# Start of the expert stages: logits with tokens on the partitions, x parts kept in x's order, the first gather split around the first gate products

## The chip, the cores and the metric

One core of one Trainium2 chip. The metric is the time of one execution on the device in microseconds; the median of the runs counts.

## The reference, cut to what matters

A network of four layers on x with 256 tokens of 1024 features, all in float32: two layers of a mixer and a mixture of experts, then two of a pooling mixer with dense feed-forward parts. The change concerns the mixture of experts of the first two:

```python
def _hier_moe(x, w_grp, b_grp, w_exp, b_exp, w_gate, w_up, w_down):
    grp_logits = (xf @ w_grp + b_grp).astype(F32)          # 4 groups
    g_idx = jnp.argmax(grp_logits, axis=-1)
    exp_logits = (xf @ w_exp + b_exp).reshape(n, N_GROUPS, EXPERTS_PER_GROUP)
    top_l, top_e = lax.top_k(in_grp, TOP_K_IN_GROUP)       # 2 of the 8 of the group
    gate = p_grp[:, None] * jax.nn.softmax(top_l, axis=-1)
    ...
    hdn = jax.nn.silu(xb @ w_gate[e]) * (xb @ w_up[e])     # 1024 -> 512
    return hdn @ w_down[e]                                 # 512 -> 1024
```

## The kernel before, in words

**Sizes.** Tokens stand in two blocks `tb` of 128, features in eight tiles of 128 (`KT`). Products that need more precision than one rounded pass split each operand into a high part (rounded, float32r) and a low part (the rest): ScalarE writes the high one, VectorE the low one, and three products are summed. `x_tok` has tokens on the partitions, `xT_parts` (`xh`, `xl`) is x turned, in parts.

**Order of the work.** Each engine runs a stream written out by hand (`pe_program`, `act_program`, `dve_program`, `pool_program`, `sp_program`, in three blocks with a barrier of all engines after pair 7 of each expert stage). Engines wait for each other by semaphores (`S.name[key]`). `Banks.open` takes the next PSUM bank of a group in turn and waits until its last user was evacuated: `A_BANKS` is 0 and 1, `B_BANKS` 4 to 7.

**From the mixer to the experts (layers 0 and 1).** VectorE normalizes block 0 and then block 1 into `x_tok`. TensorE turns each block by eight transposes (`transpose_x_pe`, L479), with four products that nobody reads ahead of block 1 (`busy_pe`, L460, 128x512 in full float32, two records each). ScalarE copies the turned halves to `xh` (L495), VectorE writes `xl` (L504). ScalarE also writes the high part of `x_tok` (`token_part_act`, L1252) in an order in which the eight features of a group are apart (`by_kk`), VectorE the low part (`token_parts_dve`, L1263). `route_pe` then computes the logits with the router weights (36 columns padded to 128) as the stationary operand and 256 tokens moving, 24 products; VectorE copies them (L1162), TensorE turns them (L1110), and a chain of small VectorE operations picks group and experts (L1165 to L1178), TensorE counts places (from `chosen_hot`), with five busy products ahead. `select_dve` (L1277) makes a 0/1 matrix `sel` that places the tokens of four experts.

**Gather (`gather_pe`).** For two pairs of experts at once, x is gathered by 32 products in four banks `q`, with the parts of `x_tok` as stationary operand and `sel` moving. ScalarE evacuates banks 0 and 2 (L1317), VectorE 1 and 3 (L1332). Then `sel` is turned (L1301) and the pair's weights are placed (`weights`). There are eight gathers in a layer; the first of a block stands ahead of its first pair.

**Pair `g` (`experts_pe`).** Gate products in two halves of four feature tiles (`paired_pe`, L1345; two experts in two column halves of the array), up products alike, the hidden rows turned (L1405), down products in two halves, and the last pair's result combined. Each half gives two weight chunks back.

**Weights.** `loads_sp` issues chunks of 1 MB in the order of use (L358), each when the last user of its slot is done; in an expert stage there are 16 slots (7 of the ring, 9 lent, the areas of `xh`, `xl` and `x_tok` among them). A pair has 12 chunks.

Of the kernel before, what the change touches and what calls it, by code (L numbers as in the profile page):

```python
# [465 lines left out]

def transpose_x_pe(e, k, n, after=None):
    S = k.S
    for tb in range(NB):
        if n < 0:  # L470
            e.wait_ge(*S.x_loaded[tb][0])
        for half in range(2):
            view = pairs(k.banks.open(e, B_BANKS, ("xT", n, tb, half))[:, :], 4)
            if n >= 0 and half == 0:
                busy_pe(e, k, k.banks["xT", n, tb, half], BUSY[after][tb])
            if n >= 0:
                e.wait_ge(*S.x_tok[n, tb, half])
            for i in range(4):
                ins = e.transpose(view[:, i, :], k.x_tok[:, tb, block(4 * half + i)], k.ident)  # L479
            ins.then_inc(*S.turned.tell((n, tb, half)))  # L480
# [617 lines left out]

def route_pe(e, k, layer, n):
    S, R = k.S, k.route  # L1100
    _, hi, lo = split_views(k, ("router", layer))
    bank = k.banks.open(e, A_BANKS, ("logits", layer))
    e.wait_ge(*S.low["router", layer])
    x_ready(e, k, n, 1)
# [6 lines left out]
    ins.then_inc(*S.product.tell(("turned_logits", layer)))  # L1111
# [10 lines left out]
def route_turned(k, bank):  # L1122
    return pairs(bank[:, 0:NB * N_LOGITS])
# [18 lines left out]
def route_dve(e, k, layer):  # L1142
# [17 lines left out]
    token_parts_dve(e, k, layer)  # L1160
    e.wait_ge(*S.used["router", layer])
    e.tensor_copy(k.rot_tmp[0:n, 0:T], k.banks["logits", layer][0:n, 0:T]).then_inc(*S.dve_out.tell(("logits", layer)))  # L1162
    view = route_turned(k, k.banks["turned_logits", layer])
    e.wait_ge(*S.product["turned_logits", layer])
    e.tensor_tensor(R.gl, view[:, :, 0:N_GROUPS], mid_bcast(k.b_grp[:, layer, :], NB), ALU.add).then_inc(*step.tell(("group_logits", layer)))  # L1165
    e.tensor_tensor(R.el, view[:, :, N_GROUPS:n], mid_bcast(k.b_exp[:, layer, :], NB), ALU.add).then_inc(*S.dve_out.tell(("turned_logits", layer)))
# [5 lines left out]
    e.wait_ge(*S.dve_out["turned_logits", layer])  # L1172
# [86 lines left out]
def token_parts_dve(e, k, layer):  # L1259
    S = k.S  # L1260
    for tb in range(NB):
        e.wait_ge(*S.token_high[layer, tb])
        e.tensor_tensor(k.x_tok_low[:, tb, :, :], by_kk(k.x_tok[:, tb, :]), k.x_tok_high[:, tb, :, :].bitcast(F32), ALU.subtract  # L1263
                        ).then_inc(*S.token_low.tell((layer, tb)))
# [21 lines left out]
def gather_pe(e, k, X, G):  # L1286

    S, b = X.S, k.experts
    for q in range(KT // 2):
        view = pairs(X.banks.open(e, B_BANKS, X.key("xg", G, q))[:, :])  # L1290
# [6 lines left out]
        ins.then_inc(*S.product.tell(X.key("gather", G, q)))  # L1297
    view = pairs(X.banks.open(e, B_BANKS, X.key("selT", G))[:, :], GATHERED)
# [36 lines left out]
def paired_pe(e, k, X, tiles, name, g, per, lhs):  # L1335

    for half in range(2):
# [48 lines left out]
def experts_pe(e, k, X, first, last):  # L1386
    S, b = X.S, k.experts
    gather_pe(e, k, X, first // GATHERED)
    for g in range(first, last):
        xg = b.xg[:, :, places(g % GATHERED)]  # L1390
        gate = X.banks.open(e, (0,), X.key("silu", g))
        if g % GATHERED == 0:
            e.wait_ge(*S.act_out[X.key("xg", g // GATHERED, 2)])
            e.wait_ge(*S.dve_out[X.key("xg", g // GATHERED, 3)])
        paired_pe(e, k, X, [gate], "gate", g, KT // 2, xg)
        up = X.banks.open(e, (1,), X.key("h", g))
        paired_pe(e, k, X, [up], "up", g, KT // 2, xg)
        if gathered_after(g, last) is not None:
            gather_pe(e, k, X, gathered_after(g, last))
# [16 lines left out]
def experts_act(e, k, X, first, last, ahead=None):  # L1416

    S, b = X.S, k.experts
    gather_act(e, k, X, first // GATHERED)
    for g in range(first, last):  # L1420
# [1525 lines left out]
```

## Time and profile before

| | |
|---|---|
| Median of 3 runs | 2324.59 us (2318.47 to 2326.11) |
| The profiled execution | span 2323.1 us from its first to its last instruction |
| TensorE busy | 2166.1 us, 93% |
| VectorE busy | 1142.2 us, 49% |
| ScalarE busy | 784.0 us, 34% |
| Moved | 622.66 MB, mean 268 GB/s |

The time of the profiled execution itself is not given beside its span; the span lies 1.5 us under the median. Busy TensorE is the time in which any matmul record is open. Two records that overlap on the array are counted once. Windows and timelines give microseconds from the first instruction.

### The profile page before, as it was taken

To read this page: it belongs to the slowest core of one execution; us is meant where nothing else is said; L and a number is where in the kernel's file an instruction comes from. 1 tells how busy PE (TensorE), PEld (TensorE's weight loads), DVE (VectorE), ACT (ScalarE), POOL (GpSimd) and SP (SyncE) were. 2 spreads that over 40 slices of the span, in tenths; PEclk is the share of its full clock that TensorE was granted. 3 is DMA by queue.
4 is the path that set the end of the run, shared out by engine and by line. 5 is a ranking of instruction groups with operands and counts; after the bars stand their busy time and mean duration, and the time that the engine had idled before them with its cause. 6 is when DMAs were issued, how large, how long until landed. Compare 5 with 4: busy or idle time off the path is not lost.

```text
span 2323.1 us, 30109 instructions
## 1 busy us (share of the span) xinstructions
PE 2166.1 (93%) x12126; PEld 1528.0 (66%) x12126; DVE 1142.2 (49%) x1786; ACT 784.0 (34%) x1299; POOL 61.5 (3%) x62
## 2 busy tenths in 40 slices
PE   8999998899887989997988999999999999989998
PEld 7884443443367944433433688898888788888887
DVE  5582222121156831211111666678666766787666
ACT  3441110111034321101111355454555455554553
POOL 0010000000010100000000000001000000001000
PEclk9999999899998799999999999999999999999999
DMA  9449999999972289999999864634555464534561
GB/s 289 145 175 379 421 421 421 417 421 420 413 246 73 76 363 420 420 421 415 420 420 421 295 209 168 199 128 127 181 200 200 154 208 166 193 96 159 167 208 46
DMA packets 231542, 622.66 MB, mean 268 GB/s; under 512 B 15456, under 2 KB 166944, under 8 KB 182112
## 3 DMA queue, kind: packets, MB, share of 16 engines
q1 hardware_dynamic: 226096, 605.32, 68.7%
q0 software_dynamic: 3040, 10.78, 1.5%
q10 hardware_dynamic: 2256, 4.50, 0.5%
q8 instruction: 102, 1.67, 0.3%
q14 instruction: 48, 0.39, 0.0%
HBM read 619.51 MB, written 1.05 MB: 267 GB/s over the span
## 4 chain that ended last, share of the span: by engine, by line
PE 41%; DMA 6%; DVE 4%; ACT 2%; issue 1%; POOL 0%; SPq 0%; DVEq 0%; ACTq 0%
PE bank L1517 14%; PE bank L1505 10%; PE bank L1518 7%; PE bank L228 6%; PE bank L1345 3%; DMA arena<-in_moe_w_up 1%; DMA ring<-in_moe_w_up 1%; DMA ring<-in_ffn_gate 1%; DMA w_parts<-in_moe_w_up 1%; DMA x_tok<-in_moe_w_up 1%; DVE w_low L439 1%; PE bank L1673 1%; ACT w_high L432 1%; DVE x_tok L687 0%; DVE x_tok L676 0%
## 5 line engine op out<-in xcount | busy, mean ns | idle before, releaser
L439 DVE TENSOR_TENSOR w_low<-ring,w_high 128x1024 fp32r<-128x1024 f32 x364 | 441.1, 1225 | 271.7 <-ACT w_high L432 271.7
L1517 PE MATMUL bank<-xT_parts,w_high 128*128 128x512 f32 x1408 | 496.2, 395 | 6.0 <-DVE xT_parts L504 6.0
L432 ACT ACTIVATE w_high<-ring 128x1024 fp32r<-128x1024 f32 x364 | 377.1, 1053 | 218.0 <-PE bank L1518 184.6
L1518 PE MATMUL bank<-xT_parts,w_low 128*128 128x256 f32 x1408 | 394.5, 280 | 0.0
L1345 PE MATMUL bank<-ring,arena 128*64 128x512 f32 x1344 | 339.0, 594 | 17.3 <-DMA w_parts<-in_moe_w_gate 5.3
L1517 PEld LDWEIGHTS bank<-xT_parts,w_high 128*128 128x128 f32 x1408 | 264.0, 188 | 69.0 <-DVE xT_parts L504 6.9
L1345 PE MATMUL bank<-w_parts,arena 128*64 128x512 f32 x768 | 263.8, 609 | 13.4 <-DMA w_parts<-in_moe_w_up 6.7
L1518 PEld LDWEIGHTS bank<-xT_parts,w_low 128*128 128x128 f32 x1408 | 265.8, 189 | 3.1
L1345 PEld LDWEIGHTS bank<-ring,arena 128*64 128x64 f32 x1344 | 110.1, 137 | 230.5 <-issue 221.9
L1453 DVE SCALAR_TENSOR_TENSOR arena<-arena,bank 128x512 f32<-128x512 f32 x32 | 23.9, 747 | 434.1 <-PE bank L1345 434.1
L228 PE MATMUL bank<-w_high,xT_parts 128*128 128x256 f32 x1152 | 222.9, 290 | 10.4 <-DVE w_low L439 8.8
L228 PEld LDWEIGHTS bank<-w_high,xT_parts 128*128 128x128 f32 x1152 | 186.4, 195 | 13.0 <-ACT arena L564 4.5
L228 PE MATMUL bank<-w_low,xT_parts 128*128 128x256 f32 x576 | 165.0, 286 | 0.0
L1345 PEld LDWEIGHTS bank<-w_parts,arena 128*64 128x64 f32 x768 | 81.1, 140 | 121.3 <-issue 117.0
L1468 DVE TENSOR_TENSOR arena_rounded<-bank,arena_rounded 128x512 fp32r<-128x512 f32 x64 | 41.2, 686 | 217.8 <-ACT arena_rounded L1438 217.8
L1505 PE MATMUL bank<-w_high,hidden_low 128*128 128x512 f32 x320 | 126.3, 395 | 0.0
L1505 PE MATMUL bank<-w_low,hidden_high 128*128 128x512 f32 x320 | 126.2, 394 | 0.0
L1505 PE MATMUL bank<-w_high,hidden_high 128*128 128x512 f32 x320 | 126.1, 394 | 0.0
L228 PE MATMUL bank<-xT_parts,w_high 128*128 128x256 f32 x608 | 115.7, 292 | 9.0 <-DVE xT_parts L504 6.0
L228 PEld LDWEIGHTS bank<-w_low,xT_parts 128*128 128x128 f32 x576 | 112.6, 195 | 0.2
L1438 ACT ACTIVATE arena_rounded<-bank 128x512 fp32r<-128x512 f32 x64 | 34.7, 594 | 229.0 <-PE bank L1345 229.0
L228 PEld LDWEIGHTS bank<-xT_parts,w_high 128*128 128x128 f32 x608 | 98.7, 199 | 10.8 <-issue 5.4
(284 smaller groups left out, 2934.4 us busy)
## 6 DMA issues: line engine op xcount, KB each, us to landing
ring<-in_moe_w_gate SPq DMA_DIRECT2D x56, 1024.0 KB, 24.3
ring<-in_moe_w_up SPq DMA_DIRECT2D x56, 1024.0 KB, 21.0
ring<-in_moe_w_down SPq DMA_DIRECT2D x56, 1024.0 KB, 25.8
ring<-in_ffn_gate SPq DMA_DIRECT2D x44, 1024.0 KB, 6.8
ring<-in_ffn_up SPq DMA_DIRECT2D x44, 1024.0 KB, 5.4
ring<-in_ffn_down SPq DMA_DIRECT2D x44, 1024.0 KB, 6.6
w_parts<-in_moe_w_up SPq DMA_DIRECT2D x32, 1024.0 KB, 26.1
w_parts<-in_moe_w_down SPq DMA_DIRECT2D x32, 1024.0 KB, 26.1
```

The source lines that it names most:

```text
L228: ins = e.matmul(out, lhs, rhs, start=first and i == 0, stop=last and i == len(parts) - 1)
L432: e.activation(hi, src, ACT.Copy).then_inc(*S.high.tell(key))
L439: e.tensor_tensor(lo, src, hi.bitcast(F32), ALU.subtract).then_inc(*S.low.tell(key))
L1345: ins = e.matmul(tile[r, :], lhs[:, half * per + kk, r], X.ring.view(chunks[j])[:, kk, BANK * n:BANK * n + BANK], start=half == 0 and kk = ...
L1438: e.activation(b.yh[:, cols], X.banks[X.key("y", g, n)][:, :], ACT.Copy).then_inc(*S.act_out.tell(X.key("y_high", g, n)))
L1453: e.scalar_tensor_tensor(out=b.silu, in0=b.silu, scalar=b.weight[:, i:i + 1], in1=X.banks[X.key("h", g)][:, :], op0=ALU.mult, op1=ALU.mult ...
L1468: e.tensor_tensor(b.yl[:, cols], X.banks[X.key("y", g, n)][:, :], b.yh[:, cols].bitcast(F32), ALU.subtract).then_inc(*S.dve_out.tell(X.key ...
L1505: ins = e.matmul(out, lhs, rhs[:, 0, cols], start=g == 0 and j == 0, stop=g == FT - 1 and j == 2)
L1517: e.matmul(pairs(bank[:, :]), hi[:, j, :], k.x_parts[:, :, j, :], start=j == 0, stop=False)
L1518: ins = e.matmul(bank[:, 0:T], lo[:, j, :], k.xh[:, j, :], start=False, stop=j == KT - 1)
L1673: ins = e.matmul(scores[:, 2 * i + blk, :], d.decayed[r, j, block(blk)], d.queries(d.decayed[r, j, block(blk)], m), start=True, stop=True)
```

## The change

Three things, in both layers. (1) `route_pe` takes over the transposes of x and computes the logits with the blocks of `xT_parts` as stationary operand and the 36 router columns moving, so that they come out with tokens on the partitions: 48 products in place of 24, those of block 0 with `xh` ahead of block 1's transposes, and no copy and turning of logits. Two busy products in place of four. (2) The parts of `x_tok` are written in x's own order, and the gather's weight loads read them eight words apart. (3) Of the first gather of each block, banks 0 and 1 come ahead of gate half 0, banks 2 and 3 ahead of gate half 1, and the turned `sel` and the weights behind the up products. One busy product stands ahead of each stage's first gather. Line numbers behind L464 grow (L479 is L478, L1345 is L1374, L1301 is L1326, L1405 is L1440).

```diff
+def transpose_block_pe(e, k, n, tb, busy=0):
...
+def logits_high_pe(e, k, layer, n, tb):
+    _, hi, lo = split_views(k, ("router", layer))
+    bank = k.banks.open(e, A_BANKS, ("logits", layer)) if tb == 0 else k.banks["logits", layer]
+    out = logits_by_token(bank)[:, tb, :]
+    e.wait_ge(*S.low["router", layer])
+    e.wait_ge(*S.x_high[n, tb, 1])
+    mm(e, out, [(k.xh[:, j, block(tb)], w[:, j, 0:N_LOGITS]) for j in range(KT) for w in (hi, lo)], last=False)
+def logits_low_pe(e, k, layer, n, tb):
+    x_ready(e, k, n, tb)
+    ins = mm(e, logits_by_token(k.banks["logits", layer])[:, tb, :], [(k.xl[:, j, block(tb)], hi[:, j, 0:N_LOGITS]) for j in range(KT)], first=False)
 def route_pe(e, k, layer, n):
-    mm(e, bank[:, 0:T], three([((hi[:, j, :], lo[:, j, :]), (k.xh[:, j, :], k.xl[:, j, :])) for j in range(KT)])
-       ).then_inc(*S.used.tell(("router", layer)))
-    view = route_turned(k, k.banks.open(e, A_BANKS, ("turned_logits", layer)))
-    e.wait_ge(*S.dve_out["logits", layer])
-    for b in range(NB):
-        ins = e.transpose(view[:, b, :], k.rot_tmp[0:N_LOGITS, block(b)], k.ident[0:N_LOGITS, 0:N_LOGITS])
+    transpose_block_pe(e, k, n, 0)
+    logits_high_pe(e, k, layer, n, 0)
+    transpose_block_pe(e, k, n, 1, 2)
+    logits_low_pe(e, k, layer, n, 0)
+    logits_high_pe(e, k, layer, n, 1)
+    logits_low_pe(e, k, layer, n, 1)
 def route_dve(e, k, layer):
     token_parts_dve(e, k, layer)
     e.wait_ge(*S.used["router", layer])
-    e.tensor_copy(k.rot_tmp[0:n, 0:T], k.banks["logits", layer][0:n, 0:T]).then_inc(*S.dve_out.tell(("logits", layer)))
 def token_part_act(e, k, n, layer, tb):
-    e.activation(k.x_tok_high[:, tb, :, :], by_kk(k.x_tok[:, tb, :]), ACT.Copy).then_inc(*S.token_high.tell((layer, tb)))
+    e.activation(k.x_tok_high[:, tb, :], k.x_tok[:, tb, :], ACT.Copy).then_inc(*S.token_high.tell((layer, tb)))
-def gather_pe(e, k, X, G):
+def gather_x_pe(e, k, X, G, first, last):
-    for q in range(KT // 2):
+    for q in range(first, last):
         if q == 0:
+            if G == 0 and X.main:
+                busy_pe(e, k, bank, 1)
...
-            ins = mm(e, view[:, i, :], [(x[:, tb, 2 * q + i, :], b.sel[:, tb, :]) for tb in range(NB) for x in (k.x_tok_high, k.x_tok_low)])
+            ins = mm(e, view[:, i, :], [(by_kk(x[:, tb, :])[:, 2 * q + i, :], b.sel[:, tb, :]) for tb in range(NB) for x in (k.x_tok_high, k.x_tok_low)])
+def gather_rest_pe(e, k, X, G):
...
 def experts_pe(e, k, X, first, last):
-    gather_pe(e, k, X, first // GATHERED)
+    gather_x_pe(e, k, X, first // GATHERED, 0, KT // 4)
...
-        paired_pe(e, k, X, [gate], "gate", g, KT // 2, xg)
+        for half in range(2):
+            if g == first and half == 1:
+                gather_x_pe(e, k, X, g // GATHERED, KT // 4, KT // 2)
+            if g % GATHERED == 0:
+                e.wait_ge(*S.act_out[X.key("xg", g // GATHERED, 2 * half)])
+                e.wait_ge(*S.dve_out[X.key("xg", g // GATHERED, 2 * half + 1)])
+            paired_pe(e, k, X, [gate], "gate", g, KT // 2, xg, (half,))
         up = X.banks.open(e, (1,), X.key("h", g))
         paired_pe(e, k, X, [up], "up", g, KT // 2, xg)
+        if g == first:
+            gather_rest_pe(e, k, X, g // GATHERED)
```

TensorE from the transposes of x to the counting of places, layer 0, before (`xT_parts` are the parts of x turned, `w_high_51` and `w_low_55` those of the router, `tables` holds the identity):

```order
L479 MATMUL bank<-tables,x_tok 128x128 x8
L460 MATMUL bank<-tables 128x512 x4
L479 MATMUL bank<-tables,x_tok 128x128 x8
L228 MATMUL bank<-xT_parts,w_high_51 128x256 x2
L228 MATMUL bank<-xT_parts,w_low_55 128x256
...
L1110 MATMUL bank<-tables,rot_tmp 128x36 x2
L460 MATMUL bank<-tables 128x512 x5
L228 MATMUL bank<-chosen_hot,tables 128x32 x5
```

The same place in the changed kernel:

```order
L478 MATMUL bank<-tables,x_tok 128x128 x8
L228 MATMUL bank<-w_high_51,xT_parts 128x36
L228 MATMUL bank<-w_low_55,xT_parts 128x36
...
L460 MATMUL bank<-tables 128x512 x2
L478 MATMUL bank<-tables,x_tok 128x128 x8
L228 MATMUL bank<-w_high_51,xT_parts 128x36 x9
L228 MATMUL bank<-w_low_55,xT_parts 128x36
...
L228 MATMUL bank<-w_high_51,xT_parts 128x36 x8
L460 MATMUL bank<-tables 128x512 x5
L228 MATMUL bank<-chosen_hot,tables 128x32 x5
L460 MATMUL bank<-tables 128x512
```

Sixteen products of block 0 moved between the two sets of transposes, and 32 stand behind them where 24 of twice the tokens and two turns stood.

TensorE from the last products of the first gather to the first down products, layer 0, before (`arena_rounded` holds `sel`, `ring` and `w_parts` hold weight chunks, `arena` the gathered x and the hidden rows):

```order
L228 MATMUL bank<-arena_rounded,x_tok_high 128x256
L228 MATMUL bank<-arena_rounded,x_tok_low 128x256
L1301 MATMUL bank<-tables,arena_rounded 128x128 x4
L228 MATMUL bank<-gate_w,arena_rounded 128x2 x4
L1345 MATMUL bank<-ring,arena 64x512 x25
...
L1405 MATMUL bank<-tables,arena 128x128 x4
L1345 MATMUL bank<-w_parts,arena 64x512 x8
```

The same place in the changed kernel, from gate half 0:

```order
L1374 MATMUL bank<-ring,arena 64x512 x8
L228 MATMUL bank<-arena_rounded,x_tok_high 128x256
L228 MATMUL bank<-arena_rounded,x_tok_low 128x256
...
L1374 MATMUL bank<-ring,arena 64x512 x17
...
L1326 MATMUL bank<-tables,arena_rounded 128x128 x4
L228 MATMUL bank<-gate_w,arena_rounded 128x2 x4
L1440 MATMUL bank<-tables,arena 128x128 x4
L1374 MATMUL bank<-w_parts,arena 64x512 x8
```

Eight gate products (half 0) moved ahead of the second sixteen gather products, and the turned `sel` and the weights moved from ahead of the gates to behind the up products.

## Rows read from the trace of the kernel before

**Rows 1.** Busy by stretch (us, busy by engine, PEclk, DMA share, GB/s); TensorE's timeline.
```profile
300.00:640.00 340.00, 307.05 (x1486) 133.68 (x1484) 63.75 (x104) 36.94 (x71) 0.00 (x0) 0.98 1.01 418
...
950.00:1290.00 340.00, 305.55 (x1482) 132.69 (x1480) 63.76 (x104) 36.92 (x71) 0.00 (x0) 0.98 1.01 418
...
415.11 0.55 PE L228 MATMUL bank<-arena_rounded,x_tok_high 128*128 128x256 f32 x1 [11.39 <-DVE arena_rounded L1277]
...
1062.33 0.55 PE L228 MATMUL bank<-arena_rounded,x_tok_high 128*128 128x256 f32 x1 [9.56 <-DVE arena_rounded L1277]
```

**Rows 2.** Busy by stretch, both holes in the stream and layer 1's gather.
```profile
189.30:194.10 4.80, 4.80 (x25) 1.66 (x26) 0.00 (x0) 1.62 (x3) 0.00 (x0) 1.00 0.12 26
...
836.80:843.00 6.20, 6.20 (x38) 3.04 (x39) 0.69 (x1) 2.21 (x4) 0.00 (x0) 1.00 0.10 21
...
831.60:835.00 3.40, 3.40 (x17) 3.40 (x18) 0.98 (x6) 0.60 (x1) 0.00 (x0) 0.52 1.01 426
```

**Rows 3.** Timeline of the weight queue (start, us, engine, line, operation).
```profile
193.00 4.24 SPq L358 DMA_DIRECT2D ring<-in_moe_w_up  x4
...
211.25 0.80 SPq L358 DMA_DIRECT2D w_parts<-in_moe_w_gate  x2
...
841.88 4.24 SPq L358 DMA_DIRECT2D ring<-in_moe_w_up  x4
...
860.16 0.80 SPq L358 DMA_DIRECT2D w_parts<-in_moe_w_gate  x2
```

**Rows 4.** Timeline of ScalarE and VectorE, layer 0.
```profile
165.26 1.09 ACT L495 ACTIVATE xT_parts<-bank 128x512 fp32r<-128x512 f32 x2 [10.37 <-PE bank L479]
...
169.61 1.32 ACT L495 ACTIVATE xT_parts<-bank 128x512 fp32r<-128x512 f32 x2 [1.29 <-PE bank L479]
...
171.57 4.15 DVE L1263 TENSOR_TENSOR x_tok_low<-x_tok,x_tok_high 128x1024 fp32r<-128x1024 f32 x2
...
176.52 0.17 DVE L1165 TENSOR_TENSOR group_logits<-bank,b_grp 128x8 f32<-128x8 f32 x1 [0.47 <-PE bank L1110]
...
186.29 0.69 DVE L1332 COPY arena<-bank 128x512 f32<-128x512 f32 x1 [1.00 <-PE bank L228]
```

**Rows 5.** Timeline of TensorE, layer 0, routing to the first down products.
```profile
165.50 3.60 PE L460 MATMUL bank<-tables 128*128 128x512 f32 x8
...
168.93 1.37 PE L479 MATMUL bank<-tables,x_tok 128*128 128x128 f32 x8
...
181.44 1.30 PE L228 MATMUL bank<-chosen_hot,tables 128*128 128x32 f32 x10 [0.46 <-DVE chosen_hot L1178]
...
184.12 0.36 PE L228 MATMUL bank<-arena_rounded,x_tok_high 128*128 128x256 f32 x1 [1.39 <-DVE place L1186]
...
187.99 0.60 PE L1301 MATMUL bank<-tables,arena_rounded 128*128 128x128 f32 x4
...
189.30 10.94 PE L1345 MATMUL bank<-ring,arena 128*64 128x512 f32 x49
...
204.31 0.72 PE L1405 MATMUL bank<-tables,arena 128*128 128x128 f32 x4 [1.05 <-DVE arena L1453]
```

**Rows 6.** The page, costliest groups (line, engine, tiles, busy, mean ns | idle before).
```profile
L439 DVE TENSOR_TENSOR w_low<-ring,w_high 128x1024 fp32r<-128x1024 f32 x364 | 441.1, 1225 | 271.7 <-ACT w_high L432 271.7
...
L432 ACT ACTIVATE w_high<-ring 128x1024 fp32r<-128x1024 f32 x364 | 377.1, 1053 | 218.0 <-PE bank L1518 184.6
```

**Rows 7.** Timeline of TensorE, layer 1.
```profile
831.51 0.55 PE L228 MATMUL bank<-arena_rounded,x_tok_high 128*128 128x256 f32 x1 [1.38 <-DVE place L1186]
...
838.18 10.94 PE L1345 MATMUL bank<-ring,arena 128*64 128x512 f32 x49
...
853.19 0.72 PE L1405 MATMUL bank<-tables,arena 128*128 128x128 f32 x4 [1.05 <-DVE arena L1453]
```

**Rows 8.** One line's instructions: duration ns min/median/max, first and last start, forms.
```profile
L1252 ACT ACTIVATE x_tok_high<-x_tok x4: 2092/2126/2168, 166.2 to 818.2; 128x1024 fp32r<-128x1024 f32 x4
...
L1405 PEld LDWEIGHTS bank<-tables,arena x128: 195/209/220, 204.3 to 1282.8; 128*128 128x128 f32 x128
```

More of the change, by code:

```diff
@@ L464 @@
 BUSY = {"mixer": (0, 4), "experts": (4, 4), "ffn": (0, 4)}
+def transpose_block_pe(e, k, n, tb, busy=0):
+    S = k.S
+    if n < 0:
+        e.wait_ge(*S.x_loaded[tb][0])
+    for half in range(2):
+        view = pairs(k.banks.open(e, B_BANKS, ("xT", n, tb, half))[:, :], 4)
+        if half == 0:
+            busy_pe(e, k, k.banks["xT", n, tb, half], busy)
+        if n >= 0:
+            e.wait_ge(*S.x_tok[n, tb, half])
+        for i in range(4):
+            ins = e.transpose(view[:, i, :], k.x_tok[:, tb, block(4 * half + i)], k.ident)
+        ins.then_inc(*S.turned.tell((n, tb, half)))
 def transpose_x_pe(e, k, n, after=None):
-    S = k.S
     for tb in range(NB):
[L470 to L480, printed above, removed]
+        transpose_block_pe(e, k, n, tb, BUSY[after][tb] if n >= 0 else 0)
 def x_parts_at(k, n, tb, half):
@@ L1093, in load_router_pool @@
     e.dma_start(k.router_wide[:, :, N_GROUPS:n], tiled_rows(k.A["moe_w_exp"][layer])).then_inc(*S.router_loaded.land(layer))
+def logits_high_pe(e, k, layer, n, tb):
+    S = k.S
+    _, hi, lo = split_views(k, ("router", layer))
[5 more added lines that the diff above has]
+def logits_low_pe(e, k, layer, n, tb):
+    S = k.S
+    _, hi, _ = split_views(k, ("router", layer))
+    x_ready(e, k, n, tb)
+    ins = mm(e, logits_by_token(k.banks["logits", layer])[:, tb, :], [(k.xl[:, j, block(tb)], hi[:, j, 0:N_LOGITS]) for j in range(KT)], first=False)
+    if tb == NB - 1:
+        ins.then_inc(*S.used.tell(("router", layer)))
 def route_pe(e, k, layer, n):
     S, R = k.S, k.route
[L1101 to L1104, printed above, removed]
-    mm(e, bank[:, 0:T], three([((hi[:, j, :], lo[:, j, :]), (k.xh[:, j, :], k.xl[:, j, :])) for j in range(KT)])
-       ).then_inc(*S.used.tell(("router", layer)))
-    view = route_turned(k, k.banks.open(e, A_BANKS, ("turned_logits", layer)))
-    e.wait_ge(*S.dve_out["logits", layer])
-    for b in range(NB):
-        ins = e.transpose(view[:, b, :], k.rot_tmp[0:N_LOGITS, block(b)], k.ident[0:N_LOGITS, 0:N_LOGITS])
-    ins.then_inc(*S.product.tell(("turned_logits", layer)))
+    transpose_block_pe(e, k, n, 0)
[4 more added lines that the diff above has]
+    logits_low_pe(e, k, layer, n, 1)
     bank = k.banks.open(e, A_BANKS, ("places", layer))
@@ L1160, in route_dve @@
     token_parts_dve(e, k, layer)
+    view = logits_by_token(k.banks["logits", layer])
     e.wait_ge(*S.used["router", layer])
[L1162 to L1164 removed]
     e.tensor_tensor(R.gl, view[:, :, 0:N_GROUPS], mid_bcast(k.b_grp[:, layer, :], NB), ALU.add).then_inc(*step.tell(("group_logits", layer)))
[L1166 removed]
+    e.tensor_tensor(R.el, view[:, :, N_GROUPS:n], mid_bcast(k.b_exp[:, layer, :], NB), ALU.add).then_inc(*S.dve_out.tell(("logits", layer)))
     first_of(R.gl, R.gmax, R.goh, k.tab("desc_grp"), N_GROUPS)
@@ L1171, in route_dve @@
     e.wait_ge(*step["barred", layer])
-    e.wait_ge(*S.dve_out["turned_logits", layer])
+    e.wait_ge(*S.dve_out["logits", layer])
     e.tensor_tensor(el8, el8, bcast(R.goh.rearrange("p a g -> p (a g)"), PER_GROUP), ALU.add).then_inc(*step.tell(("in_group", layer)))
@@ L1262, in token_parts_dve @@
         e.wait_ge(*S.token_high[layer, tb])
[L1263 to L1264 removed]
+        e.tensor_tensor(k.x_tok_low[:, tb, :], k.x_tok[:, tb, :], k.x_tok_high[:, tb, :].bitcast(F32), ALU.subtract).then_inc(*S.token_low.tell((layer, tb)))
 def select_dve(e, k, X, G):
@@ L1332, in gather_dve, with paired_pe @@
         e.tensor_copy(b.xg[:, 2 * q:2 * q + 2, :], pairs(X.banks[X.key("xg", G, q)][:, :])).then_inc(*S.dve_out.tell(X.key("xg", G, q)))
-def paired_pe(e, k, X, tiles, name, g, per, lhs):
-    for half in range(2):
+def paired_pe(e, k, X, tiles, name, g, per, lhs, halves=(0, 1)):
+    for half in halves:
         chunks = [X.key(name, g, half, j) for j in range(PAIR)]
@@ L1418, in experts_act @@
     S, b = X.S, k.experts
-    gather_act(e, k, X, first // GATHERED)
+    gather_x_act(e, k, X, first // GATHERED)
     for g in range(first, last):
@@ L1424, in experts_act @@
         e.activation(b.silu, X.banks[X.key("silu", g)][:, :], ACT.Silu).then_inc(*S.act_out.tell(X.key("silu", g)))
+        if g == first:
+            gather_rest_act(e, k, X, g // GATHERED)
         if gathered_after(g, last) is not None:
-            gather_act(e, k, X, gathered_after(g, last))
+            gather_x_act(e, k, X, gathered_after(g, last))
+            gather_rest_act(e, k, X, gathered_after(g, last))
         e.wait_ge(*S.product[X.key("hT", g)])
```

25 lines of the change are left out of this document (13 added, 12 removed).

## The prediction

> **What bounds the kernel now.** I read the busy shares by stretch first, then the weight queue, then the timeline of TensorE around the two expert stages (some 190 to 650 us and 838 to 1290 us). From 300 to 640 us and from 950 to 1290 us the DMA engines are full (share 1.01, 418 GB/s) while TensorE is busy 307.05 and 305.55 of 340 us [rows 1]. So an expert stage ends when its last weights land, and TensorE has little to spare: 32.95 and 34.45 us of idle time, of which 11.39 and 9.56 us are one wait at the block boundary after pair 7 [rows 1], during which the queue keeps moving. What remains, 21.6 and 24.9 us, is TensorE's cover.
>
> Ahead of each stage stands the one hole in this DMA stream. All slots are full, and the next load waits until the first half of gate products has given its slot back: the DMA engines are nearly idle from 189.3 to 194.1 us (share 0.12) and from 836.8 to 843.0 us (0.10) [rows 2]. The loads were issued at 193.00 and 841.88 us [rows 3], so data moves about 1.15 us after a release. A stage gets shorter by what the change takes out of DMA idle time, as long as TensorE does not become the bound, and never by more than 4.8 + 6.2 = 11 us in all.
>
> **The change, step by step, in layer 0.** Two megabytes take 5.0 us at the 418 GB/s of [rows 1]; a pair of released chunks is that much.
>
> 1. Logits. ScalarE's two copies of block 0 begin at 165.26 us and end 1.09 us later [rows 4]. The 16 high products of that block then run in what was cover. Small products with full 128-column weights: ten records with 32 columns span 1.30 us [rows 5], some 0.12 us each, so 1.9 us, to 168.4. Two busy products instead of four: eight records take 3.60 us [rows 5], so two take 1.7, to 170.1. The transposes of block 1 stood at 168.93 us [rows 5] and so come 1.2 us later, and with them ScalarE's copies, 169.61 + 1.32 us [rows 4], now to 172.1. Then 16 high and 8 low products, 2.9 us, and 0.2 us to be seen: 175.35.
> 2. VectorE has no copy of the logits and no turned logits to wait for. Its two low parts took 4.15 us with a stride [rows 4]; contiguous ones are like the split of a weight part, 1225 ns by the page's row of L439 [rows 6]: 2.45 us. It is free at the same 175.35. The group logits stood at 176.52 us [rows 4]: **1.2 us gained**.
> 3. From there to the first gather nothing is added. The one new busy product (0.86 us) lies in a wait of 1.39 us [rows 5]. The gather starts at 182.95 instead of 184.12.
> 4. The gather in halves. Before, gates began 5.18 us after the gather (184.12 to 189.30 [rows 5]), and the evacuations were hidden under the turning of the selection and the weights, 1.3 us from 187.99 us [rows 5]. Now the first half takes 1.9 us, and then TensorE waits for VectorE's copy of the second bank, which ended 186.29 + 0.69 us, 2.9 us after the gather's start [rows 4]. Gates begin at 185.95, **3.35 us earlier**, and the first release comes at 189.65. Data moves from 190.8: the hole is 1.5 us instead of 4.8.
> 5. The second half has the same bare evacuation: 1.9 + 1.0 us ahead of gate half 1, whose release comes at 196.0; the first two chunks have run out at 195.8, so the DMA engines idle again until 197.15, 1.35 us. So far 2.0 us gained.
> 6. The rest of the gather (1.3 us) now stands behind the up products, and VectorE's product waits for its weights, 0.45 us more. From the gather's start to the turning of the hidden rows I get 2.95 + 3.43 + 2.9 + 3.43 + 6.86 + 1.3 + 0.45 + 0.9 = 22.3 us, where 20.2 stood (184.12 to 204.31 [rows 5]): **2.1 us lost**, 0.9 net of the start. The release that stood at 211.25 us [rows 3] comes at 212.2, data at 213.4. The queue before had work to 194.15 + 20 = 214.15, now to 212.15. Its next data moves 0.75 us earlier than before. That is layer 0's gain, **0.75 us**.
>
> Layer 1: the same chain, but its gather ran from 831.51 us with TensorE at 0.52 of its clock in 831.6 to 835.0 [rows 2, 7], that is at 1.2 GHz for most of it, and the gates only started at 838.18 us [rows 7]. With a busy product just ahead I take it at 2.4 GHz: gather at 830.35, gates at 833.35, release 4.85 us earlier, at 837.05, data at 838.2 (idle 1.4 instead of 6.2); the second hole 1.35; the later release 860.16 us [rows 3] half a microsecond earlier (853.19 [rows 7] becomes 852.7), and a third hole of 1.25. 6.2 - 4.0 = **2.2 us**.
>
> At the two block boundaries the same halving costs TensorE 2.1 us each, under 21.6 and 24.9 us of cover: nothing. Turned bank order in the A group: nothing, its earlier users were evacuated long before. The sum is **3.0 us faster**: 2320.1 us for the profiled execution (span 2323.1 us), which lies 1.5 us under the median of the runs, 2324.59; so 2321.6 us. What this kernel's measurement can tell from no change is about 0.3%, 7 us.
>
> The unknown price is the gather's weight load. Its 128 columns are now read 8 words (32 bytes) apart. The nearest rows go two ways. ScalarE reading x with this stride takes 2126 ns against 1053 for a contiguous tile of the same size, VectorE 4.15 us for two against 1.22 for one [rows 4, 6, 8]: a factor 1.7 to 2. TensorE's own rows at a stride of 4 words are four transposes in 0.72 us, where four contiguous ones take 0.60 [rows 5]: (0.72 - 0.28 for the last one) / 3 = 0.15 us apart against 0.11, at 209 ns per load [rows 8]. I take the second side, since it is the same engine and operation, and its contiguous end, 0.12 us per product as before; at 0.15 each half of a gather is 0.5 us longer and the sum 2 us smaller, 1.0 us faster. The other end is 0.235.
>
> **Rivals.**
>
> *A. The strided load sets the pace (slower).* At 0.235 us a gather's 32 products take 3.75 us more. The first delays the gates; but all eight gathers of a layer stand in TensorE's stream, 29.9 us. Layer 0: 29.9 + 0.9 + 2.1 (boundary) - 21.6 of cover = 11.3 us; layer 1: 29.9 - 0.5 + 2.1 - 24.9 = 6.6 us; together 18 us slower, 2342.5. It decides where eight gathers use up the cover, at 2.1 to 2.9 us each, 0.19 to 0.21 us per product. For it speak both other engines, which slow down alike at this stride; against it, TensorE's pace at half the stride. The Trainium skill (SBUF — State Buffer, on SBUF "cachelines" in the section Door 1) says that an access in a new 16-byte line pays a penalty and that one can stride for free over 4 fp32 words; 8 are beyond that. By this rule the weight loads would slow down, as the rows of ScalarE and VectorE agree with it, and the sum would be this rival's.
>
> *B. The clock falls in the logits.* From 164.6 to 175.1 us TensorE would do transposes, 48 products of 36 columns and two busy ones, where it did four busy ones and 256-column products. Before the fall at 831.6 us [rows 2] it had done ten 32-column records and waited. If the logits run at 1.2 GHz, some 19 products take 0.12 us more and the chain to the gather is 2.4 us longer in each layer: layer 0 slower by 1.65 us, layer 1 by 0.15: 1.8 us slower, 2326.4. The Trainium skill (TensorE: Matmul & The Clock Gate, Part 4: PE-mode transpose) states that transposes do not count as activity for the clock; that would favour this case, and the time by it is the same.
>
> *C. More of the holes goes.* If the down products of the first pairs stay at 2.4 GHz, their release is some 1.7 us earlier and step 5 and its counterpart in layer 1 alone limit: 2.0 + 3.5 = 5.5 us, 2319.1. If every hole closed, 11 us, 2313.6. The bare evacuations speak against the last.
>
> *D. Nothing moves.* The time to the stage's end would be given by something else than the stream; 2324.6. The full DMA share speaks against it.
>
> **How the numbers follow.** My forecast has 0.39, A 0.22, B 0.13, C at 2319 0.12 and with most holes closed 0.09, D 0.05. The likeliest case alone spans 2316 to 2327 us. The range is to hold 8 in 10: down to 2314, near the largest gain, up to 2342, where A's full price begins. Faster by over 0.3% needs more than 7 us and so most of the holes, with some of the spread of the runs (2318.47 to 2326.11): 0.12. Slower by over 0.3% is A, and a little of B with a smaller A: 0.23. The same: 0.65.
>
> **What would show it.** Right: gates start 3 to 3.5 us earlier in layer 0 and near 833 us in layer 1; two or three DMA holes of 1 to 1.5 us each instead of one of 5 or 6; hidden rows turned a microsecond later in layer 0; gather products 0.12 us apart. Wrong: gather products over 0.19 us apart with TensorE never waiting for weights after 300 us (A); a granted clock of 0.5 between 170 and 178 us (B); a stage from first gates to last weights that is no shorter in DMA idle time although the holes are gone (D).

## The result, and the profile after

| | before | changed |
|---|---|---|
| Median of the runs | 2325.07 us (2318.47 to 2326.11, 4 runs) | 2352.39 us (2346.8 to 2359.53, 4 runs) |
| Ratio, with its 95% interval | 1 | 1.0126 [1.0113, 1.014] |
| Profiled execution: time, span | span 2323.1 us | 2351.46 us, span 2349.4 us |
| TensorE busy | 2166.1 us, 93% | 2230.9 us, 95% |
| VectorE busy | 1142.2 us | 1139.0 us |

The changed kernel is **slower by 1.3%, 27 us**. The forecast was 3 us faster, and the range ended at 2342. The first look is at the two stretches in which the DMA stream had set the pace (busy by engine, PEclk, DMA share, GB/s), beside [rows 1]:

```profile
300.00:640.00 340.00, 323.75 (x1482) 148.78 (x1478) 62.16 (x102) 37.38 (x72) 0.00 (x0) 0.97 1.00 413
950.00:1290.00 340.00, 324.75 (x1486) 156.85 (x1484) 64.94 (x106) 38.41 (x75) 0.00 (x0) 0.97 1.00 414
```

TensorE's busy time rose by 16.7 and 19.2 us, with practically as many records. One line names the cause, the weight loads of the gather (duration ns min/median/max), with the two copies that lost their stride; below it the same loads of the kernel before:

```profile
L228 PEld LDWEIGHTS bank<-arena_rounded,x_tok_high x256: 312/339/344, 181.1 to 1261.6; 128*128 128x128 f32 x128
...
L1270 ACT ACTIVATE x_tok_high<-x_tok x4: 1058/1060/1061, 163.3 to 831.7; 128x1024 fp32r<-128x1024 f32 x4
L1281 DVE TENSOR_TENSOR x_tok_low<-x_tok,x_tok_high x4: 1216/1217/1218, 171.3 to 833.7; 128x1024 fp32r<-128x1024 f32 x4
```

```profile
L228 PEld LDWEIGHTS bank<-arena_rounded,x_tok_high x256: 186/189/336, 184.1 to 1225.2; 128*128 128x128 f32 x128
```

339 ns instead of 189, and the products start 0.24 us apart instead of 0.12. What stands on the other side are TensorE's waits in 300 to 640 us (us in total, times, longest), before:

```profile
PE bank L228 <- DVE arena_rounded L1277: 11.4, 1, 11.4
PE bank L1345 <- DMA w_parts<-in_moe_w_up: 2.9, 3, 1.3
PE bank L1345 <- DMA w_parts<-in_moe_w_gate: 2.7, 2, 1.4
PE bank L1345 <- DMA ring<-in_moe_w_up: 2.6, 2, 1.3
```

and after:

```profile
PE bank L228 <- DVE arena_rounded L1294: 9.5, 1, 9.5
PE bank L1374 <- issue: 2.6, 3, 0.9
PE bank L228 <- DVE arena_rounded L1506: 1.6, 1, 1.6
```

Waits on DMA added up to 16.5 us there (18.4 in 950 to 1290 us), and no such wait is left in either stretch. TensorE has become the bound of the expert stages. Its timeline at the start of layer 0, beside [rows 5], shows the chain of the steps 1 to 6:

```profile
165.63 3.36 PE L460 MATMUL bank<-tables 128*128 128x512 f32 x4
168.83 1.04 PE L478 MATMUL bank<-tables,x_tok 128*128 128x128 f32 x8
...
181.13 0.51 PE L228 MATMUL bank<-arena_rounded,x_tok_high 128*128 128x256 f32 x1 [0.40 <-DVE arena_rounded L1294]
...
186.22 3.65 PE L1374 MATMUL bank<-ring,arena 128*64 128x512 f32 x16 [0.94 <-DVE arena L1361]
189.80 0.51 PE L228 MATMUL bank<-arena_rounded,x_tok_high 128*128 128x256 f32 x1
...
194.79 7.48 PE L1374 MATMUL bank<-ring,arena 128*64 128x512 f32 x33 [0.83 <-issue]
...
205.25 0.66 PE L1326 MATMUL bank<-tables,arena_rounded 128*128 128x128 f32 x4
...
208.06 0.72 PE L1440 MATMUL bank<-tables,arena 128*128 128x128 f32 x4 [1.37 <-DVE arena L1491]
```

The place of every microsecond is read best with fixed marks: the start of VectorE's last scaling of `x_tok` ahead of the routing ("scale"), and the turning of the hidden rows of pair n ("h n"), each taken from the timelines. Us between marks:

| | to scale | to h0 | to h7 | to h8 | to h15 | to scale | to h0 | to h7 | to h8 | to h15 | to end |
|---|---|---|---|---|---|---|---|---|---|---|---|
| before | 168.1 | 36.2 | 186.6 | 45.9 | 196.3 | 182.4 | 37.7 | 186.8 | 44.6 | 197.9 | 1040.6 |
| changed | 165.2 | 42.9 | 192.4 | 53.1 | 192.5 | 180.4 | 47.6 | 192.2 | 52.3 | 192.6 | 1038.1 |

Starts of a layer cost 6.7 and 9.9 us, first blocks 5.8 and 5.4, the boundaries after pair 7 7.2 and 7.7; the second blocks give back 3.8 and 5.3. The rest, 7.4 us less, is the parts before, between and behind. Sum 26.3 us, the difference of the spans. How much of the 7.4 us the change gave is not shown: in the four traces whose code is the same up to the first mark (before, and the three with products that nobody reads) it lies between 164.3 and 168.3 us.

In the changed kernel the time from one h to the next is 23.4 us in every pair without a gather and 32.5 (34 for the first of a block) in every pair with one. Before it was 23.4 and 28.5 (up to 30.2 for the first of a block), but the last three pairs of layer 0 took 34.9, 25.8 and 29.9 us: there TensorE waited for weights. With nothing to wait for, h0 to h15 would have taken 6 x 28.5 + 8 x 23.4 + 46 = 404 us, and 429 were taken. **The cover was 25 us.** Six strided gathers within the blocks cost 4.0 us more each, 24 us; the seventh stands in the boundary, where the stride alone costs 0.1 and 1.6 us (46.0 and 46.2 with edit (2) alone, 45.9 and 44.6 before). That is the whole cover: what else was added then had none left. This is the theory that the runs below tested.

### The profile page after: what moved, and what is told of

It is laid out like the page before. It is cut to its first block, busy times and chain, and to the rows that moved or that the text cites. A ratio compares the mean times of both kernels' runs of the same rounds, so it can differ in the third digit from the quotient of the medians.

```text
span 2349.4 us, 30202 instructions
## 1 busy us (share of the span) xinstructions
PE 2230.9 (95%) x12166; PEld 1586.9 (68%) x12166; DVE 1139.0 (48%) x1784; ACT 779.2 (33%) x1299; POOL 62.4 (3%) x62
## 4 chain that ended last, share of the span: by engine, by line
PE 47%; DVE 4%; ACT 2%; issue 1%; POOL 0%; DVEq 0%; ACTq 0%
PE bank L1555 14%; PE bank L1543 9%; PE bank L1374 7%; PE bank L228 7%; PE bank L1556 7%; DVE w_low L439 1%; PE bank L1711 1%; ACT w_high L432 1%; DVE x_tok L691 0%; DVE x_tok L680 0%; DVE bn L669 0%; DVE acc L1778 0%; PE bank L478 0%; DVE acc L1626 0%; PE bank L460 0%
## 5 line engine op out<-in xcount | busy, mean ns | idle before, releaser
L1374 PE MATMUL bank<-ring,arena 128*64 128x512 f32 x1344 | 345.0, 607 | 7.1 <-issue 5.2
L1555 PEld LDWEIGHTS bank<-xT_parts,w_high 128*128 128x128 f32 x1408 | 263.9, 187 | 68.5 <-DVE xT_parts L508 6.9
L1374 PE MATMUL bank<-w_parts,arena 128*64 128x512 f32 x768 | 263.5, 611 | 3.4 <-issue 3.4
L1374 PEld LDWEIGHTS bank<-ring,arena 128*64 128x64 f32 x1344 | 112.5, 140 | 221.9 <-issue 219.6
L228 PE MATMUL bank<-w_high,xT_parts 128*128 128x256 f32 (+1 forms) x1216 | 236.4, 290 | 12.0 <-DVE w_low L439 8.8
L228 PEld LDWEIGHTS bank<-w_high,xT_parts 128*128 128x128 f32 x1216 | 198.4, 197 | 15.1 <-issue 5.8
L228 PE MATMUL bank<-w_low,xT_parts 128*128 128x256 f32 (+1 forms) x608 | 173.3, 287 | 0.0
L1374 PEld LDWEIGHTS bank<-w_parts,arena 128*64 128x64 f32 x768 | 81.1, 141 | 112.3 <-issue 112.3
L228 PE MATMUL bank<-arena_rounded,x_tok_high 128*128 128x256 f32 x256 | 107.0, 418 | 21.0 <-DVE arena_rounded L1294 19.9
L228 PEld LDWEIGHTS bank<-w_low,xT_parts 128*128 128x128 f32 x608 | 119.8, 197 | 0.2
L228 PE MATMUL bank<-xT_parts,w_high 128*128 128x256 f32 x576 | 106.8, 288 | 6.2 <-DVE w_low L439 3.2
```

The source lines that it names most:

```text
L228: ins = e.matmul(out, lhs, rhs, start=first and i == 0, stop=last and i == len(parts) - 1)
L1374: ins = e.matmul(tile[r, :], lhs[:, half * per + kk, r], X.ring.view(chunks[j])[:, kk, BANK * n:BANK * n + BANK], start=half == 0 and kk = ...
L1555: e.matmul(pairs(bank[:, :]), hi[:, j, :], k.x_parts[:, :, j, :], start=j == 0, stop=False)
```

## The experiments

Fourteen kernels ran; "before" was timed beside each group (medians 2323.01, 2325.17, 2325.09 and 2323.02 us).

**Stride by itself.** To the kernel before, 108 products were appended behind its last, twelve at each of nine steps.

```diff
+    for step in (1, 2, 3, 4, 5, 7, 8, 9, 16):
+        for i in range(12):
+            e.matmul(view[:, 0:T], x[:, 0:step * P].rearrange("p (a s) -> p s a", s=step)[:, 0, :], k.xh[:, 0, :], start=True, stop=True)
```

> The kernel before with 108 products appended behind the last feed-forward part: twelve each (float32r, 128x128 weights, 256 columns moving, same moving operand) with the weight columns 1, 2, 3, 4, 5, 7, 8, 9 and 16 words apart. Nothing reads their result. Theory (the stride sets TensorE's pace): 0.12 us apart at 1 word and about 0.24 at 8, as the gather of the changed kernel shows; 16 like 8. Where between 1 and 8 it begins, and whether 7 and 9 behave like 8, tells distance from bank or line. Rival (the gather slowed down for another reason, such as the two parts' place in memory or traffic of the weight stream): 0.12 us at every step.

Starts of the loads, from the timeline, all at the full clock: 0.120 us apart at 1 and 2 words, 0.174 at 3, 0.233 at 4, 0.229 at 5, 0.234 at 7, 0.241 at 8 and 9, 0.225 at 16. Over all of them (duration ns min/median/max; one run, 2339.28 us with these products on top):

```profile
L2676 PEld LDWEIGHTS bank<-xT_parts x108: 188/321/341, 2314.6 to 2336.3; 128*128 128x128 f32 x108
L2676 PE MATMUL bank<-xT_parts x108: 278/393/408, 2314.9 to 2336.4; 128*128 128x256 f32 x108
```

The price rises up to a step of 4 words and is flat beyond; a step of 2 is free. The four turns of hidden rows, at 4 words [rows 5], gave 0.15 us apart, which is not what a stream of loads pays at that step.

**Edit (2) alone**: the kernel before with x parts in x's order.

> The kernel before with the parts of x_tok in x's order and the gather's strided weight loads, and nothing else of the change. Theory (the strided load is the whole loss): gather products 0.24 us apart, TensorE without waits for weights from 300 us on, and 1.0% to 1.3% slower, 2350 to 2355 us. Rival (the split gather, its bare evacuations and the small logits products carry a good part): clearly less, 0.4% to 0.8% slower, with the rest found in the runs of the other parts.

2327.6 us, ratio 1.0021 [1.001, 1.0032]: under both ranges, the theory's (1.0% to 1.3%) and the rival's (0.4% to 0.8%). Alone, the slower load costs little. Products are 0.24 us apart, there is no wait on DMA to speak of (0.3 and 0), and h0 to h15 take 428.3 and 431.3 us against 428.8 and 429.3: 404 + 24 is 428. Its windows show both engines at their limit:

```profile
300.00:640.00 340.00, 326.71 (x1516) 152.15 (x1514) 65.07 (x106) 37.98 (x73) 0.00 (x0) 0.98 1.01 418
950.00:1290.00 340.00, 326.94 (x1512) 150.90 (x1510) 65.07 (x106) 37.97 (x73) 0.00 (x0) 0.97 1.01 419
```

**The change without edit (2)**: the parts as before, logits by tokens and halves kept.

> The changed kernel with the parts of x_tok in the order of before, so that the gather's weight loads are contiguous; logits by tokens, split gather and busy products stay. Theory (the strided load is the whole loss): gather products 0.12 us apart, TensorE waits for weights again after 300 us (some 15 us a layer), and the time is what the forecast's sum said, 1 to 5 us under before (2319 to 2324 us). Rival (halves and logits cost too): 5 us or more above before.

2325.01 us, 1.0016 [1.0006, 1.0026]; waits on DMA 9.9 and 16.1 us. The loss is gone, but the 1 to 5 us of gain that the theory still had did not come. The boundary of layer 0 takes 53.1 us here too, and the second block behind it 188.8 instead of 196.3; in layer 1 the boundary takes 46.6. So the two pieces alone cost 0.2% each, and together 1.26%: costs don't add, they share one cover.

**Half of the loads strided**: low parts as before.

> The changed kernel with the low part of x_tok in the order of before and only the high part strided: 16 of a gather's 32 weight loads are contiguous. Theory (cover first, loss beyond it): 1.9 us more per gather, 15 us a layer, lies under the 17 to 21 us of TensorE's waits, so that most of it costs nothing: within 6 us of the kernel with contiguous loads. Rival (every strided load costs its time): half the loss, some 13 to 15 us above it.

2330.34 us, 1.0034 [1.002, 1.0047], waits 1.9 and 5.4 us. That is 5.3 us above the kernel with short loads, within the theory's 6 and not the rival's 13 to 15: the first half of the strided loads costs 0.18%, the second half 0.92%.

**The edits one after another, on top of the strided loads.** First the changed kernel with the whole first gather ahead again:

```diff
-    gather_x_pe(e, k, X, first // GATHERED, 0, KT // 4)
+    gather_x_pe(e, k, X, first // GATHERED, 0, KT // 2)
+    gather_rest_pe(e, k, X, first // GATHERED)
```

> The changed kernel with the whole first gather (all 32 products, places and weights) ahead of the gates again: strided weight loads and logits by tokens stay. Theory (the cover is spent by the strided loads, and it is the halves that are then paid in full): from hidden rows of pair 7 to those of pair 8 it takes 46 us again instead of 53.1 and 52.3, from first gather to first hidden rows 24.2 us instead of 26.9 and 29.2; together 14 + 8 = 22 us come back, 2330 us, ratio 1.001 to 1.004, with no TensorE wait on DMA left in either window. Rival (the logits by tokens and their cold clock are what is paid): boundaries go to 46 as well, since no logits stand there, but the starts keep their extra, and the sum is 2335 to 2342 us, ratio 1.005 to 1.008.

2335.09 us, 1.0035 [1.0022, 1.0049]: boundaries 48.2 and 45.9, gather to h0 24.2 in both layers, as the theory had it. The time lies on the edge of the rival, and part of it may be right: from scale to h0 the two layers take 40.9 and 42.7 us, with edit (2) alone 41.0 and 39.5. Starts that no edit touched differ by 2.3 us between traces (36.2 to 38.5), so that these 3 us are not shown to be the logits.

Then split at the layers' starts only:

> The changed kernel, but split only at the start of a layer; at the block boundary the whole gather comes first. Theory: the two boundaries are 46 us again instead of 53.1 and 52.3, and without cover all of it is seen: 2352 - 14 = 2338 us, ratio 1.005 to 1.007. Rival (the transfers, late by the slow first block, set the second block's time): TensorE waits for DMA in place of the boundary's loss, 2346 to 2352 us, ratio over 1.009.

2338.51 us, 1.0068 [1.0051, 1.0084], as expected; boundaries 48.1 and 46.3. So with the strided loads in place the steps are +0.21%, logits +0.14% (about the width of the intervals, so not clear of nothing), halves at the starts +0.33%, halves at the boundaries +0.58%.

**The same edits where the cover is whole.** Logits by tokens and their busy products alone, then the halves alone:

> Logits by tokens with their busy products alone: parts of x in the old order (weight loads 0.12 us apart), whole first gather ahead of the gates. Theory: TensorE's chain at a layer's start changes by at most 1 us, boundaries stay at 46, TensorE still waits 16 us for DMA in each window, and what is lost at a start is taken from those waits: 2325 us, ratio 0.999 to 1.001. Rival (the chain from logits to gather is what sets the layer's time): a clock that falls in the logits costs 2 us a layer in full, 2329 us, ratio 1.0015 to 1.003.

2326.39 us, 1.0007 [0.9997, 1.0017]; waits on DMA 17.2 and 17.7 us. Its boundaries take 49.7 and 44.3 us: the first is 4 us longer than the 45.9 of before, with the clock low for 17.1 us instead of 10.2, although no edit touches it.

> The kernel before with the split first gather alone (at layer starts and at the block boundaries). Theory: boundary 53 us instead of 46 and 45, first gather to hidden rows 24 us instead of 20 to 22, but TensorE's waits for DMA behind the boundary shrink by as much: 2326 us, ratio 1.000 to 1.002. Rival (costs simply add): 2 x 7 us at the boundaries and 2 x 4 at the starts are seen in the time, 2345 us, ratio 1.009.

2325.71 us, 1.0003 [0.9995, 1.0012]; boundaries 50.9 and 46.7 us, waits 13.9 and 15.8 us. What costs 0.91% without cover costs nothing that can be measured with it.

**How large is the cover?** Products that nobody reads, in the banks of every second gather of the kernel before:

```diff
         if q == 0:
...
+            for i in range(33 if G % 2 else 0):
+                e.matmul(view[:, 0, :], k.x_tok_high[:, 0, i % KT, :], b.sel[:, 0, :], start=True, stop=True)
```

> The kernel before, with 33 products more (weight loads of adjoining words) in every second gather, 4 of 8 in a layer: 4 us each, 16 us a layer. TensorE's own time from the hidden rows of pair 0 to those of pair 15 is 6 x 28.5 + 8 x 23.4 + 46 = 404 us where nothing waits for a transfer, and 429 are taken. Theory (a cover of 25 us there, to be used up before anything shows): 429 us again, 2325 us, ratio 0.999 to 1.002. Rival (TensorE's time is worth something all along, as a sum): 16 us more in each layer, 2357 us, ratio 1.014.

2324.94 us, 1.0004 [0.9995, 1.0012]; h0 to h15 430.0 and 429.7 us, with 16 us of work more in each layer. With 66 products:

> As the one with 33 products more, with 66: 8 us in every second gather, 32 us a layer. Theory (cover of 25 us): 404 + 32 = 436 us instead of 429 from the hidden rows of pair 0 to those of pair 15, 7.5 us more in each layer, 2340 us, ratio 1.005 to 1.008. Rival 1 (a sum): 2389 us, 1.028. Rival 2 (the cover is only what the windows show as waits, 17 us): 15 us more in each layer, 2355 us, ratio 1.013.

2333.6 us, 1.0046 [1.0033, 1.0059], just under the theory's range; h0 to h15 435.6 and 435.8, where 436 was worked out. The cover is 25 us in a layer, more than the windows' waits on DMA.

**TensorE's time or the strides?** The changed kernel without the gather's low products, so that the gathered x lacks its low part:

> The changed kernel with only the high parts of x in the gather (its low products are left out): 16 strided loads 0.24 us apart take what 32 took before, everything else is as in the changed kernel. Theory (it is TensorE's time that counts, not the strides as such): TensorE waits for DMA again, some 10 to 17 us in each window, the halves' cost at boundaries and starts is hidden as in the kernel with the old order of the parts, 2327 us, ratio 1.000 to 1.003. Rival (strided reads hold up the transfers or the other engines too): stays above 1.006.

2325.74 us, 1.0008 [0.9998, 1.0018]. The loads are as slow as in the changed kernel, but half as many, and the waits are back:

```profile
L228 PEld LDWEIGHTS bank<-arena_rounded,x_tok_high x256: 312/338/345, 182.3 to 1227.9; 128*128 128x128 f32 x128
...
PE bank L1374 <- DMA w_parts<-in_moe_w_up: 4.0, 3, 1.3
PE bank L1374 <- DMA arena<-in_moe_w_up: 2.6, 2, 1.3
```

Strided reads do not hold up the transfers (with all of them, at the boundary of layer 0, the DMA share is 1.01 from 417.9 to 434.8 us); they take TensorE's time.

**A layout that keeps both.** Pairs of columns: loads read every second word, the copies read runs of two.

```diff
+def by_twos(v):
+    return v.rearrange("q (a p i) -> q a p i", a=KT // 2, i=2)
...
+            ins = mm(e, view[:, i, :], [(by_twos(x[:, tb, :])[:, q, :, i], b.sel[:, tb, :]) for tb in range(NB) for x in (k.x_tok_high, k.x_tok_low)])
```

> The changed kernel with the parts by tokens in pairs of columns, so that a weight load reads every second word and the parts are cut from runs of two words. The products appended to the kernel before were 0.12 us apart at a step of 2 words as at 1. Theory: gather products 0.12 us apart, the rest of the change as it is, 2328 us, ratio 1.001 to 1.003; VectorE's part takes between 1.2 and 4.2 us. Rival (any stride in the gather costs): 0.24 us apart and above 1.01.

2325.08 us, 1.0005 [0.9993, 1.0017], and the load as fast as at adjoining words:

```profile
L228 PEld LDWEIGHTS bank<-arena_rounded,x_tok_high x256: 193/195/335, 182.5 to 1229.0; 128*128 128x128 f32 x128
```

ScalarE's copy takes 1166 ns and VectorE's 1216, so they keep their gain too. This one edit of the changed kernel takes its whole loss away.

**What the boundary's 7 us are.** Eighteen busy products were meant for the wait of 9.5 us ahead of the second block's gather.

```diff
+            if G == CUT // GATHERED and X.main:
+                busy_pe(e, k, bank, 18)
```

> The changed kernel with 18 busy products in TensorE's wait of 9.5 us for the second block's selection, 0.43 us each at the full clock, 7.7 us in all, so that they fit in the wait. Theory (of the 7 us that a boundary takes longer, about half is the clock: 16 gate loads of the first half took 6.5 us at the low clock where the same half takes some 3.3 at the full one; the rest is two bare evacuations and stays): the granted clock stays full from the wait to the gates, the boundary takes 49 to 50 us instead of 53, 2 x 3.5 us less, 2345 us, ratio 1.008 to 1.011. Rival (it is the evacuations and the second gather alone): stays at 53, ratio 1.012 to 1.014.

2378.77 us, 1.0239 [1.0226, 1.0253]: a miss of my reading. The timeline of all engines there:

```profile
418.79 2.22 PE L228 MATMUL bank<-arena_rounded 128*128 128x512 f32 x8 [1.64 <-DVE arena_rounded L1508]
...
429.12 0.34 SPq L358 DMA_DIRECT2D x_low_slot<-in_moe_w_gate  x1
429.12 0.76 DVE L1294 TENSOR_TENSOR arena_rounded<-tables,rank 128x256 fp32r<-128x256 f32 x2 [6.96 <-issue]
...
429.91 0.50 PEld L460 LDWEIGHTS bank<-tables 128*128 128x128 f32 x2 [9.33 <-issue]
429.91 1.22 PE L460 MATMUL bank<-tables 128*128 128x512 f32 x1 [8.90 <-issue]
```

SyncE, VectorE and TensorE all begin again at 429.1 to 429.9 us. The wait is not for the selection, as its releaser had said; it is the barrier of all engines between two blocks of the program. The products stood behind it, as work on top, and each is two records of 0.43 us, as "two records each" in the description said and my expectation forgot. The first gather product came 16.7 us later, at 446.6. That is a dose too: with no cover, the boundaries grew by 13.8 and 17.5 us. Layer 0's grew by 2.9 us less than it got, and its clock was low for 10.2 us instead of 17.1; in layer 1 it was low for 17.1 as before, and nothing came back.

The clock is read more directly from the changed kernel, at the wait and in two windows of 16 and 17 gate records (third column TensorE busy, then PEclk, DMA share, GB/s last):

```profile
417.90:434.80 16.90, 10.22 (x30) 5.91 (x32) 1.45 (x3) 0.60 (x1) 0.00 (x0) 0.50 1.01 407
...
428.90:435.30 6.40, 6.39 (x16) 1.88 (x16) 0.00 (x0) 0.00 (x0) 0.00 (x0) 0.55 1.02 420
440.34:443.80 3.46, 3.46 (x17) 1.41 (x19) 0.00 (x0) 0.00 (x0) 0.00 (x0) 1.00 0.92 384
```

At 1.2 GHz the first gate half takes 6.4 us, at 2.4 GHz 3.5: 3 of the 7 us. An evacuation that nothing covers, 0.94 and 0.83 us ahead of the gate halves, makes another 1.8. Strided gather products are 0.24 us apart at either clock. Ordered by the time at the low clock, the boundaries of the kernels with the normal amount of work take 44.3 to 47.8 us with 10.2 us of it, 45.9 to 52.6 with 13.7, 48.9 to 53.1 with 17.1, 52.1 to 53.6 with 20.5. The split as such is seen in layer 1 where the low time is 10.2 us and the loads are short: 46.6 to 46.9 us with it (three kernels), 44.3 to 44.6 without (four), 2.0 to 2.6 us, which is what the prediction had priced. Why one kernel gets 10.2 us of low clock and another 17.1 is open.

**Can a split gain at all?** Parts as before, and the turned selection and the weights right behind the first half, where they cover the evacuation:

> The changed kernel with the parts of x in the old order, and in the split gather the rest (selection turned, weights) right behind the first half of the gather, where its products cover the evacuation. Can this beat the kernel before? Theory (the transfers set the layer's time, and they start again when the first gates are done; gates start as late as with the whole gather less 1.9 us, and their second half no earlier): DMA's idle time at a layer's start 4.5 to 6 us as before, 2325 us, ratio 0.999 to 1.002. Rival (the start of a layer is a chain that counts in full, so 2 us less to the first gates are gained in each layer): 2321 us, ratio under 0.999.

2326.12 us, 1.0013 [1.0004, 1.0022]: no gain, as its theory had it. No version that ran is faster than the kernel before.

## Why the prediction was wrong

**The step that failed is the price of the weight load**, "I take the second side, ... 0.12 us per product as before", with 0.235 as the other end. It measured 0.24, so that rival A is what happened. The choice went by the wrong neighbour: four turns at 4 words, too few to show a pace, against two other engines that both took twice as long at 8 words. The Trainium skill (SBUF — State Buffer, Door 1, the part on cachelines) had it as a penalty for reads in a new 16-byte line, with full bandwidth only from two hits in a line on. The appended products agree: 2 words apart (two hits) is free, 4 words apart (one hit) costs the full price, and beyond the pace is flat at 0.22 to 0.24 us. They do not agree with its next sentence, that one strides for free up to 4 fp32 words: 3 cost 0.05 us a product, and 4 the full 0.11.

With loads at 0.12 us the rest of the change costs 0.16% instead of 1.26%, so this term decides. The second term that failed is "nothing" for what the halves cost: it holds only under a cover that the load at 0.24 us uses up.

**Rival A's size was off too**, 18 us instead of 27. Its price of the gathers (29.9 us for eight; at 4.0 us each they are 32) and its cover (21.6 and 24.9 us; 25) were near. Too small were what it added for the starts and the boundaries. Scale to h0 grew by 6.7 and 9.9 us, where its terms give 3.75 + 0.9 = 4.7 and 3.75 - 0.5 = 3.3. From h0 to h15 it grew by 9.2 and 7.8 us, where its seven gathers and 2.1 less the cover give 6.7 and 3.4. That is 15.6 us more than its sum, of which the 7.4 us of the rest took half away.

By the steps of the working, in layer 0:

1. Logits: "1.2 us gained" became none. From scale to the group logits it is 8.37 us, before 8.40. The two busy calls took 3.36 us, as long as four had (3.60), since they ran at 1.2 GHz (165.0 to 168.5 us). That is rival B's clock, in another place.
2. VectorE's parts: 1217 ns each, right.
3. The busy product in the routing's wait: right in layer 0 (7.56 us from group logits to gather, before 7.60), wrong in layer 1 (9.52, before 7.60), at the low clock from 834.1 to 840.9 us. From scale to the first gather layer 1 takes 18.4 us, before 16.0: the 2.4 us of rival B, in this layer.
4. Gates 2.95 us after the gather: 5.09, since sixteen strided products take 16 x 0.24 = 3.8 us. With the old order it was 4.33 and 3.10 us, with the halves alone 3.96 and 4.49; the evacuation of 1.0 was right (0.94).
5. The holes in the stream: not one of 1.5 and one of 1.35 us. In the 40 us around them the DMA share is 0.79 in layer 0 (182 to 222 us) and 0.69 in layer 1 (846 to 886), before 0.89 and 0.85 (185 to 225, 832 to 872). Against the full 1.01 that is idle time of 8.8 and 12.8 us, where 4.8 and 6.4 were. The weight queue beside [rows 3]:

```profile
189.91 9.38 SPq L358 DMA_DIRECT2D ring<-in_moe_w_up  x4
201.91 3.76 SPq L358 DMA_DIRECT2D ring<-in_moe_w_down  x3
...
214.88 0.80 SPq L358 DMA_DIRECT2D w_parts<-in_moe_w_gate  x2
```

   The first release is 3.1 us earlier than before by the clock of the trace, 0.2 us counted from scale.
6. Gather to hidden rows in 22.3 us: 26.93. The slower loads of the two halves are 3.9 us of it; with the old order it was 24.18 and 22.94 us, so the step itself was 1 to 2 us short, the low clock among them. In layer 1 of the changed kernel it took 29.2 us, before 21.7; the gates that were to run at 2.4 GHz from 833.35 us on began at 850.12, at 1.2 GHz (847.7 to 854.5 us).

The two boundaries, "2.1 us each, ... nothing", cost 7.2 and 7.7. What the forecast called the bound, the stream, did hold for the kernel before and for every variant of the change with loads of one or two words: they all lie within 0.2% of it. That a shorter start shortens the layer, the forecast's premise, stays untested: from scale to h0 no variant of the change is clearly shorter than before (37.3 us at the least, before 36.2 and 37.7).

## What to carry to other kernels

Price an edit with the cover that the rest of the same change leaves, not with the cover of the profile before. A layout that saves about 1 us on each of eight copies can cost 0.12 us on each of 512 weight loads: count the readers first, and try the layout between (here pairs of words). And measure the cover as the difference between an engine's own time over a whole stage and the time taken, from the regular period of its steps; waits in a window show only part of it.

## What the hardware showed that I had not expected

- A weight load of 128 fp32 columns costs the same at a step of 1 and 2 words, 1.45 times at 3, and about twice from 4 words on (0.120, 0.120, 0.174, 0.233 us apart), up to 16.
- Strided loads set the same pace at either clock, 0.24 us apart at 1.2 GHz (from 422.9 us on) and at 2.4 GHz (182.2 us on). Products with short loads are 0.21 us apart at 1.2 GHz (before, from 415.5 us on) and 0.12 at 2.4 GHz, so that the stride costs 0.03 us a product at the low clock and 0.12 at the full one.
- The page's releaser of a long wait can be the first signal behind a barrier. The check is whether the other engines stand still as well.
- 16 us of additional TensorE work per layer, 32 in all, changed the time by 0.04% [-0.05, 0.12], and 64 us in all by 0.46%.
